# Thirty-two unused columns behind a table of constants, in a two-block transformer kernel on one core

## The reference

```
for grp in range(N_GROUPS):
    hid = (silu(einsum('td,edf->tef', h, w_gate[grp]))
           * einsum('td,edf->tef', h, w_up[grp])) * combine[:, grp, :, None]
    y = y + einsum('tef,efd->td', hid, w_down[grp])
```

## The kernel before, in words

| tile | first byte in the partition | remainder by 512 | by 256 |
|---|---|---|---|
| consts | 16512 | 128 | 128 |
| ring (all 8 places) | 27648 | 0 | 0 |
| residual | 93184 | 0 | 0 |
| arena | 101376 | 0 | 0 |
| square_junk | 223680 | 448 | 192 |

## Time and profile before

### The profile page before, as it was taken

How to read it: one execution, slowest core, us unless ns; L and a number is a source line. 1 busy time by engine, 2 the same in 40 slices (tenths; PEclk the granted TensorE clock), 3 DMA queues, 4 the chain that set the end, 5 groups by cost and what they waited for, 6 DMA issues and landing times. The chain is left out here.

```text
span 795.1 us, 13968 instructions
## 1 busy us (share of the span) xinstructions
PE 742.2 (93%) x5673; PEld 539.8 (68%) x5673; DVE 443.9 (56%) x772; ACT 321.3 (40%) x554; POOL 44.0 (6%) x39
## 2 busy tenths in 40 slices
PE   8999999899989999887876899999999999999998
PEld 5979976564646656544544587666548788888886
DVE  3899765544642331230330589688385865776665
ACT  4666433411432340340340664588432434343431
POOL 1000021001000000000000032301100000000000
PEclk9999999999999999998999999999999999999999
DMA  8894449988989999999999996610025445664201
GB/s 279 294 368 160 159 156 405 333 338 313 418 327 415 410 418 418 414 418 415 420 420 410 399 281 231 219 40 2 1 106 212 160 159 185 224 221 165 106 1 54
DMA packets 106387, 208.17 MB, mean 262 GB/s; under 512 B 7861, under 2 KB 55254, under 8 KB 98526
## 3 DMA queue, kind: packets, MB, share of 16 engines
q1 hardware_dynamic: 105406, 205.19, 68.8%
q10 hardware_dynamic: 864, 2.18, 0.8%
q0 software_dynamic: 64, 0.05, 0.0%
HBM read 206.31 MB, written 1.08 MB: 261 GB/s over the span
## 5 line engine op out<-in xcount | busy, mean ns | idle before, releaser
L2654 DVE TENSOR_TENSOR unit_parts<-ring,unit_parts 128x2048 fp32r<-128x2048 f32 x33 | 75.5, 2289 | 58.9 <-ACT unit_parts L1964 58.9
L1964 ACT ACTIVATE unit_parts<-ring 128x2048 fp32r<-128x2048 f32 x33 | 62.9, 1912 | 73.9 <-PE psa L1323 43.0
L1038 PE MATMUL psv<-ring,arena 128*32 128x256 f32 x960 | 60.9, 410 | 15.4 <-DMA ring<-in_w_up_dram 13.1
L1322 PE MATMUL psv<-column_parts,unit_parts 128*128 128x512 f32 (+1 forms) x192 | 65.5, 389 | 1.6 <-DVE arena L2742 1.4
L1322 PE MATMUL psa<-column_parts,unit_parts 128*128 128x512 f32 (+1 forms) x192 | 65.1, 388 | 0.0
L1038 PEld LDWEIGHTS psv<-ring,arena 128*32 128x32 f32 x960 | 34.2, 118 | 37.4 <-issue 22.6
L1323 PE MATMUL psv<-column_parts,unit_parts 128*128 128x256 f32 (+1 forms) x192 | 52.0, 271 | 0.0
L1323 PE MATMUL psa<-column_parts,unit_parts 128*128 128x256 f32 (+1 forms) x192 | 52.0, 271 | 0.0
L2785 POOL TENSOR_TENSOR small<-small,consts 128x2 f32<-128x2 f32 (+4 forms) x15 | 28.2, 1884 | 381.8 <-DVE small L2488 239.8
L1770 ACT ACTIVATE arena<-psv 128x256 f32<-128x256 f32 x8 | 3.1, 383 | 100.1 <-PE psv L1038 100.1
L1322 PEld LDWEIGHTS psv<-column_parts,unit_parts 128*128 128x128 f32 x192 | 36.1, 188 | 9.3 <-DVE unit_parts L2654 1.5
(11 more groups left out here) (441 smaller groups left out, 1688.7 us busy)
## 6 DMA issues: line engine op xcount, KB each, us to landing
ring<-in_w_gate_dram SPq DMA_DIRECT2D x43, 1024.0 KB, 9.3
ring<-in_w_up_dram SPq DMA_DIRECT2D x39, 1024.0 KB, 5.1
arena<-in_w_down_dram SPq DMA_DIRECT2D x32, 1024.0 KB
ring<-in_w_mod_dram SPq DMA_DIRECT2D x24, 1024.0 KB, 7.8
ring<-in_w_in_dram SPq DMA_DIRECT2D x23, 1024.0 KB, 10.0
ring<-in_w_down_dram SPq DMA_DIRECT2D x11, 1024.0 KB, 7.2
ring<-in_w_out_dram SPq DMA_DIRECT2D x8, 1024.0 KB, 8.0
arena<-in_w_in_dram SPq DMA_DIRECT2D x8, 512.0 KB, 16.3
```

What stands on the lines that cost most here:

```text
L1038: mm = pe.matmul(mG[32 * e:32 * e + 32, f0:f0 + FF], XT[:, k, 32 * e:32 * e + 32], w, start=(k == 0), stop=(k == KD - 1))
L1322: pe.matmul(both_parts(bank, t_0, t_1), hi, col_parts[:, :, k, t_0:t_1], start=(k == 0), stop=False)
L1964: act.activation(unit_parts[q % 3][:, 0, :], slot_of(NPRE + u_), ACT.Copy).then_inc(upper_done, 1)
L2654: vec.tensor_tensor(lo, slot_of(NPRE + at["mlp"] + 3 * n + kind), hi, ALU.subtract).then_inc(lower_done, 1)
```

## The change

The table gets one more piece, `margin`, of zeros and as many columns as bring its width to a multiple of 128: 2784 columns become 2816, so 32 are added, 128 bytes in a partition. Nothing reads them. The tile `consts` takes its width from the table, so `ring` and all that is placed behind it begin 128 bytes later. No instruction is added, taken away or moved on any engine; the load of the constants (L1410) has 2672 columns where it had 2640, and in main memory the table's rows step 11264 bytes where they stepped 11136.

More of the change, by code:

```diff
@@ L131, in constants @@
     put("epsk", np.full((P, 1), EPS))
+    put("margin", np.zeros((P, -sum(c.shape[1] for c in cols) % 128)))
     return np.ascontiguousarray(np.concatenate(cols, 1).astype(np.float32)), at
```

## The result

| | before | after |
|---|---|---|
| median of four runs | 795.38 us (794.82 to 796.22) | 805.41 us (804.82 to 808.33) |
| profiled execution, its own time | 796.86 us | 804.82 us |
| its span | 795.1 us | 803.0 us |

The ratio of the two kernels is 1.0121, with a 95% interval of 1.0099 to 1.0143: 10.0 us more, where I had forecast no change with a chance of 0.86. The case that came is rival 1 (803.8 us), to which I gave 0.09.

The account below looks back on a forecast made before the run. DMA packets were taken to bound the expert passes and TensorE the later part. Packets 0, instructions 0 and table 0.04 us on 796.86 gave 796.9, less 1.5 for the median: 795.4 us, range 793.7 to 797.1.

Parts of the forecast that it names:

- rival 1: Expert passes: each packet landing 128 bytes off pays 4.7 ns for dead bytes, 8.4 us in seven passes, 803.8 us; chance 0.09.
- What bounds the kernel: Expert passes of 31.19 to 31.56 us last as long as their DMA packets; TensorE sets the time later (600 to 700 us).
- what the change moves: Ring and arena already begin at multiples of 512 bytes; the change puts them 128 bytes past one.
- An instruction's price: TensorE products and ScalarE splits reading shifted places: 0 us, with a bound of 1.4 us both ways.
- The table's: Load of the constants around 26 us: 128 more bytes in each of 128 packets, 0.04 us.
- A packet's price at a place that is 128 bytes off: Weight loads landing 128 bytes off: 0 ns a packet, read from half places loaded at 418 GB/s.
- The bound that I put on this row: Rounding of 418 GB/s by half a unit, 0.12% of seven passes of 31.4 us: 0.3 us either way.
- The second reading: Constants landing 192 bytes past a multiple of 256, packets of 10560 bytes: 397 ns from aligned sizes, at most 401 measured.
- a second fixed part of 10 ns: Far bound for 8192, 2048 and 512 byte packets cut in two: 2.6 us a pass, 18 us in seven.
- it decides in the passes alone: Claim that dearer packets lengthen the kernel only in the expert passes, since no cover is left there.
- TensorE's wait for up weights: Sign in the expert passes: it would grow from 13.1 us by what the passes grew.
- The rule I weighed: DMA transactions of 256 bytes must start at a multiple of 256; each off packet would pay for 128 bytes more.

Follow-up runs that it names:

- the table alone: Kernel before with the constants table 32 columns wider in main memory only, the tile on the chip unchanged: 796.74 us, ratio 0.9992.
- The loads alone: Separate kernel without the computation, loading weights in five packet sizes to places on a multiple of 256 bytes and 128 bytes past one: 311.01 us, run once.
- the second experiment: Kernel before with the tile `consts` 32 columns wider on the chip, the table in main memory unchanged: 806.17 us, ratio 1.0118.

## Why the prediction was wrong

**What bounds the kernel** was right: passes last as long as their packets, and 1.2 us more of packets made each pass 1.1 us longer. So was **what the change moves**: it takes the places off a multiple and puts none on one.

**An instruction's price** of 0 held: medians of 281 and 379 ns are equal, the splits went from 1908 to 1912 and stayed at 1917 ns. **The table's** 0.04 us held as far as 0.2% can tell: 0.9992 with the table alone.

**A packet's price at a place that is 128 bytes off** is the step that failed: I took 0 ns, and it is 5. I read it from the earlier trace rows, two transfers of 4096-byte packets, 2.5 us long, behind megabytes of aligned ones. The rows are right and hold for what they are, since such a half is free where it stands; my error was to take their rate for that of a long run of the same kind. The loads alone show that a run of 4096-byte packets off its multiple goes free for about 6 us, and only then takes 163 to 164 ns (a stretch from within either part):

```profile
66.70:71.50 4.80, 0.00 (x0) 1.00 1.03 421
74.30:86.90 12.60, 0.00 (x0) 1.00 1.02 408
```

The bound that I put on this row, 0.3 us, was the rounding of 418 GB/s, a bound on the reading and not on what the row stands for. The second reading, had the same fault: a few us of packets, behind aligned units of `w_in`. Besides, "at most 401 ns" beside 397 left room for 4 ns, nearly all of rival 1's 4.7. What I did write beside it, that no row shows 8192, 2048 and 512 bytes at such a place and that a second fixed part of 10 ns is the far bound, was a price of the right kind and of twice the size; I then left it out of the forecast's range.

**Rival 1** named the right packets and nearly the right sum, 8.4 us against 10.0, by a wrong mechanism. It priced 128 bytes at 4.7 ns, by luck near the fixed 5 ns; at 32 and at 224 bytes off it fails. And "it decides in the passes alone" was wrong: 2.5 us came before them, 1.8 of it with the loads of `w_mod`, where DMA's share was 1.05 before, as the stretch from 115 us shows. I had looked only for stretches in which TensorE's digit falls. The passes gave 7.1 of the 8.4 us, which at the 1.11 us of the four measured ones is 6.4 passes' worth, where I had taken seven at 1.2. Nor did TensorE's wait for up weights grow by what the passes grew, as I had written for this rival: it grew by 2.9 us.

**The rule I weighed** (the Trainium skill, DMA: Bandwidth & Descriptors, How a descriptor splits into AXI transactions) says of what a transaction reads that a start past a multiple of 256 costs by the bytes before it. On the side that is written the runs agree on the 256: a shift by 256 bytes is free. They don't agree on the size, which is the same for 32, 128 and 224 bytes, and they show no cost at all at the start of a run. The earlier trace rows tested the side that is read, which this change leaves alone: in the kernel after, the units of `w_in` are the same rows as before and now move

```profile
44.50:47.50 3.00, 3.00 (x27) 3.00 (x27) 2.79 (x7) 2.40 (x2) 0.00 (x0) 1.00 1.10 350
```

350 GB/s where they moved 386; with the tile alone made wider (the second experiment) they move 350 too. So it is the place that is written that sets this price.

## To carry to other kernels

Before a stretch that DMA bounds, look at where the destination of each transfer begins on the chip, the base of the tile included, and put it at a multiple of 256 bytes. Rounding up a tile's width is not enough: where the tile itself begins off such a multiple, what lies behind it does too. A rate read from a short stretch bounds only short stretches: ask what ran before it and for how long the new case would run. Where DMA is the bound of a stretch, a few ns a packet are read best as share x engines x time over packets.

No version here beats the kernel before: all its long runs of weights already begin at multiples of 256 bytes, and 0, 256 and 512 bytes of shift give the same time.

## What the runs showed of the hardware

- A packet that lands at a place off a multiple of 256 bytes takes about 5 ns more, if such packets come in a long run: 310 to 315 ns for 8192 bytes, 160 to 164 for 4096, 84 to 89 for 2048, 46 to 52 for 1024 (386 to 350 GB/s), 27 to 32 (34 in the loads alone) for 512. For 2048 bytes it is the same at 32, 128 and 224 bytes past the multiple, and so is the kernel's time. As rates that is 2% for 8192 bytes, 5% for 2048 and 16% for 512 (347 to 290 GB/s).
- At the start of such a run the price is not there. In the loads alone it came on after about 10.7 us of 8192-byte packets, 6.5 us of 4096, 3 us of 2048 and 1.4 us of 512, and it was gone within an aligned MB. Something that holds work in flight and fills slowly would do this; that is only argued, and no run looks inside.
- Where a matrix product or a split reads its operand, at 0 or 128 bytes past the multiple, made no difference that a median shows.
